# Delta stage: the sum of k's squares from two dense-format products, one state step later

## The chip, the cores and the metric

The kernel runs on one core of a Trainium2 chip. The metric is the device time of one execution in microseconds (us). A program of this size was executed three times for the median, and once more under the hardware profiler.

## The reference, cut to what matters

Two blocks follow each other on 512 rows of 1024 features; only the first layer of the first block, a gated delta rule over 8 heads, is touched. For each head the reference takes q, k and v from a projection, a causal convolution of 4 taps and a silu, and then

```python
def _l2norm(t):
    return t * lax.rsqrt(jnp.sum(t * t, axis=-1, keepdims=True) + EPS)
...
k = _l2norm(qkv[..., A_QK_WIDTH:2 * A_QK_WIDTH].reshape(bsz, seq, A_HEADS, A_HEAD_K).astype(f32))
v = qkv[..., 2 * A_QK_WIDTH:].reshape(bsz, seq, A_HEADS, A_HEAD_V).astype(f32)
...
v_new = u_c - jnp.einsum("bhcd,bhdv->bhcv", w_c, state)
o_c = jnp.einsum("bhcd,bhdv->bhcv", qd, state) + jnp.einsum("bhcj,bhjv->bhcv", a_c, v_new)
state = state * dec[..., None, None] + jnp.einsum("bhcd,bhcv->bhdv", ke, v_new)
```

The sum of k's squares over the 128 features of a head is what the change computes in another way.

## The kernel before, in words

Features lie on the partitions and the 512 positions along the rows. Large products split weight and activation into a high part, rounded to the dense format `F32R`, and a low part (the rest), and add three products (high by high, high by low, low by high). A weight tile comes by DMA into `wraw`, ScalarE casts its high part (`cast`), VectorE subtracts to get the low part (`low`), and each tile is 24 matmuls of 128x512.

The delta stage has a prologue and then one turn of `delta(i)` for each of 8 heads: a hardware loop for heads 1 to 5, written out for 0, 6 (`last_qkv`) and 7 (`last`). Each engine has its own list of instructions, in an order written by hand, and works through it strictly in turn; semaphores tie the lists together. In turn i TensorE solves the triangular systems of head i (`levels`), then goes through four chunks of 128 positions (t = 0 to 3), each of which needs the state that the last one left. The gaps of both are filled with matmuls of projection tiles (`strips`, L613). The lists `BEFORE_STATE`, `AFTER_KS`, `AFTER_V` and `AFTER_S` say how many filler matmuls follow each step; whatever is left of the 48 is done after the state steps, so their number in a turn is fixed.

A state step t > 0 goes round four engines' lists like this:

- TensorE: k by state (L784) and state by q (L785), fillers, then `tt` by `rr` (L792); later `kend` by `vn` (L803) and `vn` by the decayed products (L804), fillers.
- VectorE: `rr` (L1976) after L784; the new `state` (L1987 for t = 0, L1990 after) after L803.
- ScalarE: `vn` (L1354) after L792, which releases L803.

Between these steps VectorE and ScalarE do the work for head i+1. ScalarE scales the newest tap of each convolution (`conv_newest`, L1254), applies silu, squares k into `sq[:, 1, :]` (`square_k`, L1268), casts a weight tile (L1170), switches its table (L1365), exponentiates the decay (L1308) and takes the inverse root of the sum for k (`k_norms`, L1302, L1304). VectorE adds the three older taps (`conv_older`, L1782) and prepares the decay exponents (`exponent`, L1859). The sum of k's squares itself is `sums_of_k` (L692 to L695): one float32 matmul of a matrix of ones (`ones`) by `sq[:, 1, :]` into `pa[:, 1, :]`, which the trace records as two passes of 128x512. It stands behind L792 in step t = 1, where `AFTER_V[1]` is 0:

```python
                    if t == 1 and not last:
                        sums_of_k(i + 1)
                    if not last:
                        fill(after_v[t])
```

For head 0 the same function is called alone, ahead of the first strips, and in VectorE's list the fitting place is between L1842 and `conv_older(-1, 3, 0)`:

```python
            sums_of_k(0)
            strips(s, 0, (0, 1), 0, 3 * KD)
```

Later in the prologue TensorE turns k (L700), forms the products of k and q (L712), turns v (L706), spreads the small systems (L718) and starts `levels(0)` with L733, which waits for VectorE's `tn`.

The names that matter below: `rqk` holds the inverse root, `kn` (L1849) the unit k, `state_ready`, `r_ready`, `vn_ready`, `v_done` the semaphores of the state steps.

Of the kernel before, what the change touches and what calls it, by code (L numbers as in the profile page):

```python
# [13 lines left out]
F32 = mybir.dt.float32  # L14
# [5 lines left out]
P = 128  # L20
# [104 lines left out]
def build(nc, xT, w8, w11, w_gates, consts, vecs, a_log, dt_bias, rel_flip, ln_gb, w_spat, b_spat, outT,  # L125
# [5 lines left out]
    with ctx:  # L131
# [31 lines left out]
        def ev(name):  # L163

            if name not in made:
                made[name] = ctx.enter_context(nc.semaphore(name))
            return made[name]
# [30 lines left out]
        o_hi = r.sb("o_hi", [P, HA, S], F32R)  # L198
        o_lo = r.sb("o_lo", [P, HA, S], F32R)
        ys = r.sb("ys", [P, 4, S])  # L200
        sq = r.sb("sq", [P, 2, S])
        rqk = r.sb("rqk", [P, S])
        own = Region(r.at)
        r.at += 3 * P * 4
# [17 lines left out]
        tt = r.sb("tt", [P, NC, P])  # L222
        xm = r.sb("xm", [P, NC, P])
        xm32 = r.sb("xm32", [P, NC, 32])
        kend = r.sb("kend", [P, NC, P])
        bv = r.sb("bv", [P, NC, P])
        rr = r.sb("rr", [P, NC, P])
# [348 lines left out]
        def _(pe):  # L576
# [114 lines left out]

            def sums_of_k(i):  # L692

                pe.wait_ge(ev("k_squared"), i + 1)
                mm(pa[:, 1, :], ones, sq[:, 1, :], start=True, stop=True).then_inc(ev("k_sums"), 1)  # L695

            def turn_k(i):
                pe.wait_ge(ev("kn_ready"), i + 1)
# [63 lines left out]
            def delta(i, last, last_qkv=False):  # L762
# [17 lines left out]
                for t in range(NC):  # L780
                    q = slice(t * P, t * P + P)
                    if t > 0:
                        pe.wait_ge(ev("state_ready"), i * (NC - 1) + t)
                        mm(pb[:, q], kn[:, q], state[:], start=True, stop=True).then_inc(ev("ks_done"), 1)  # L784
                        mm(acc[:, 2, q], state[:], qe[:, q], start=True, stop=False)  # L785
                        if t == 3 and last:
                            pe.wait_ge(ev("q_squared"), i + 1)
                            mm(pd[:], ones, sq[:, 0, :], start=True, stop=False)
                        if not last:
                            fill(after_ks[t])  # L790
                        pe.wait_ge(ev("r_ready"), i * (NC - 1) + t)
                        mm(pc[:, q], tt[:, t, :], rr[:, t, :], start=True, stop=True).then_inc(ev("v_done"), 1)  # L792
                    else:
                        mm(pc[:, q], tt[:, t, :], bv[:, t, :], start=True, stop=True).then_inc(ev("v_done"), 1)
                    if t == 1 and not last:
                        sums_of_k(i + 1)
                    if not last:
                        fill(after_v[t])
                    elif t in (1, 2, 3):
                        fill(1)  # L800
                    pe.wait_ge(ev("vn_ready"), i * NC + (t + 1))
                    if t < NC - 1:
                        mm(pd[:, q], kend[:, t, :], vn[:, t, :], start=True, stop=True).then_inc(ev("s_done"), 1)  # L803
                    m = mm(acc[:, 2, q], vn[:, t, :], gd[:, t, 1, :], start=(t == 0), stop=True)  # L804
                    if t == NC - 1:
                        m.then_inc(ev("o_done"), 1)
                    if not last:
                        fill(after_s[t])
# [354 lines left out]
        def _(act):  # L1163
# [102 lines left out]
            def square_k(i):  # L1266
                act.wait_ge(ev("qkv_silu"), i * 3 + 5)
                A(sq[:, 1, :], ys[:, 1, :], ACT.Square).then_inc(ev("k_squared"), 1)  # L1268

            def square_q(i):  # L1270
                act.wait_ge(ev("qkv_silu"), i * 3 + 1)
# [5 lines left out]
            gates = pb[:, 0:64].rearrange("p (t c) -> p c t", c=16)  # L1277
            A(t0[:], gates[:, 0:8, :], ACT.Exp, scale=-1.0).then_inc(ev("gate_act"), 1)
            act.wait_ge(ev("consts_landed"), 32)
            conv_newest(1, 0, -1)  # L1280
            act.wait_ge(ev("gate_dve"), at(GATE_DVE, "gate_abs"))
            A(t1[:], t1[:], ACT.Exp, scale=-1.0).then_inc(ev("gate_act"), 1)
# [52 lines left out]
            def delta(i, last, last_qkv=False):  # L1335
# [19 lines left out]

                vn_of(0)
                if not last:
                    square_k(i)
                    conv_newest(3, i + 1, i)
                    act.wait_ge(acc_done, s.number(i, 3) + 1)  # L1360
                    cast(o, 0, 2) if last_qkv else cast(s, i + 1, 1)
                vn_of(1)
# [194 lines left out]
            def stick():  # L1557
# [12 lines left out]
                for step in range(blocks + 3):  # L1570
# [15 lines left out]
                    if step < blocks:  # L1586
                        k = 3 - v
                        g = slice(SEG[k], SEG[k] + (4 - k) * P)
                        act.wait_ge(ev("z_masked"), step + 1)
                        A(sw[:, :, g], zs[:, :, g], ACT.Abs).then_inc(ev("z_abs"), 1)  # L1590
                        act.wait_ge(ev("z_abs"), step + 1)
                        A(sw[:, :, g], sw[:, :, g], ACT.Exp, scale=-1.0).then_inc(ev("z_exp"), 1)
                        act.wait_ge(ev("z_exp"), step + 1)
                        A(sw[:, :, g], sw[:, :, g], ACT.Ln, bias=1.0).then_inc(ev("z_ln"), 1)
                    if 0 < i < SBP and v == 0:
                        turned_v(i)
                        cast_ahead(s, i, 2, i == SBP - 1)
# [106 lines left out]
        def _(dve):  # L1704
# [135 lines left out]
            dve.wait_ge(ev("solve_dve"), 7)  # L1840
            ts_(en[:], e8[:], -1.0, None, ALU.mult).then_inc(ev("solve_dve"), 1)
            nc.vector.memset(yx[:, :, 0:1], 1.0).then_inc(ev("solve_dve"), 1)  # L1842
            conv_older(-1, 3, 0)


            def unit_qk(i):

# [68 lines left out]
            def delta(i, last, last_qkv=False):  # L1916
# [55 lines left out]
                for t in range(NC):  # L1972
                    q = slice(t * P, t * P + P)
                    if t > 0:
                        dve.wait_ge(ev("ks_done"), i * (NC - 1) + t)
                        stt(rr[:, t, :], pb[:, q], nbe[:, i, t:t + 1], bv[:, t, :], ALU.mult, ALU.add  # L1976
                            ).then_inc(ev("r_ready"), 1)
                        if t == 1 and not last:
                            conv_older(i, 3, i + 1, (2, 3))
                        if t == 2 and last_qkv:  # L1980
                            low_after(o, 2, 1)
                        elif t == 2 and not last:
                            low(s, i + 1, 1)
                    if t < NC - 1:
                        dve.wait_ge(ev("s_done"), i * (NC - 1) + (t + 1))
                        if t == 0:
                            nc.vector.tensor_copy(state[:], pd[:, q]).then_inc(ev("state_ready"), 1)  # L1987
                        else:
                            dve.wait_ge(ev("state_ready"), i * (NC - 1) + t)
                            stt(state[:], state[:], ecl[:, i, t:t + 1], pd[:, q], ALU.mult, ALU.add  # L1990
                                ).then_inc(ev("state_ready"), 1)
                        if t == 0 and not last:
                            conv_older(i, 3, i + 1, (1,))
                        if t == 1 and not last:
                            exponent(i + 1)
# [230 lines left out]
            def stick():  # L2226
# [19 lines left out]
                for step in range(blocks + 3):  # L2246
# [7 lines left out]
                    if 1 <= step < blocks + 1:  # L2254
                        k = 3 - (step - 1) % NC
                        g = slice(SEG[k], SEG[k] + (4 - k) * P)
                        dve.wait_ge(ev("z_ln"), step)
                        x = stt(sp[:, :, g], zs[:, :, g], 0.0, sw[:, :, g], ALU.max, ALU.add)
                        if k < 3:
                            x.then_inc(ev("sp_whole"), 1)  # L2260
# [266 lines left out]
```

## Time and profile before

| what | us |
|---|---|
| median of 3 executions | 1793.81 |
| lowest, highest | 1793.61, 1793.97 |
| the profiled execution's own time | 1793.58 |
| its span, first to last instruction | 1791.9 |
| TensorE busy | 1761.8 (98%) |
| VectorE busy | 1153.6 (64%) |
| ScalarE busy | 845.8 (47%) |
| mean granted clock of TensorE | 0.998 |

A busy TensorE is the union of its records, whose ends are modelled; a matmul record is longer than its share of the engine, since neighbours overlap. What a matmul costs is read from the distance between starts, or from the chain of waits, which counts each moment once. The profile names TensorE's array PE, its weight loads PEld, VectorE DVE, ScalarE ACT and GpSimd POOL. "idle before <- X" is the time in which the engine stood before that instruction, and X is what ended it.

The eight heads span roughly 56 to 360 us of the 1791.9; the rest of the program is not touched except for three semaphores of the second block's attention that become one (`z_steps`), with the same waits.

### The profile page before, as it was taken

The page shows a single profiled execution, that of the slowest core. Times are in us where ns is not written, and L with a number is a line of the kernel's source. Part 1 is how long each engine was busy: PE and PEld are TensorE (multiplying, and loading weights), DVE is VectorE, ACT ScalarE, POOL GpSimd, SP SyncE. Part 2 cuts the span into 40 slices and gives each one's busy share as a digit, 9 for nine tenths or more (in the row PEclk, how much of TensorE's full clock was granted, in tenths as well). Part 3 has the DMA queues.
Part 4 walks back from the last instruction along what each step waited for, and adds up shares of the span by engine and source line. Part 5 has one row for each costly group of instructions (what it writes and reads, how often), then busy time and mean ns, then how long its engine had stood idle before and what let it go on. Part 6 is the DMA issues. An engine that isn't in the chain of part 4 may idle for free.

```text
span 1791.9 us, 23591 instructions
## 1 busy us (share of the span) xinstructions
PE 1761.8 (98%) x8174; PEld 1388.8 (78%) x8174; DVE 1153.6 (64%) x1826; ACT 845.8 (47%) x1311; POOL 34.4 (2%) x61
## 2 busy tenths in 40 slices
PE   9999999899999999999999999999999999999998
PEld 6787777678888888888887788888887765677886
DVE  7888888567777743377777677776433556665444
ACT  6555555444444432267777444444322465643222
POOL 1000000000000000000000000000000000100000
PEclk9999999999999999999999999999999999999999
DMA  5522122022222142143331222222321312223221
GB/s 198 167 70 70 59 70 59 36 96 95 93 94 93 59 155 88 62 132 106 103 114 65 94 94 94 94 94 84 124 97 52 106 36 71 92 78 99 100 93 60
DMA packets 45816, 163.26 MB, mean 91 GB/s; under 512 B 5841, under 2 KB 8164, under 8 KB 45760
## 3 DMA queue, kind: packets, MB, share of 16 engines
q1 hardware_dynamic: 40864, 148.00, 24.7%
q0 software_dynamic: 4464, 14.47, 2.9%
q8 instruction: 32, 0.52, 0.1%
q14 instruction: 24, 0.20, 0.0%
q10 hardware_dynamic: 432, 0.07, 0.0%
HBM read 155.89 MB, written 6.63 MB: 91 GB/s over the span
## 4 chain that ended last, share of the span: by engine, by line
PE 91%; DVE 4%; ACT 3%; issue 1%; DMA 0%; SPq 0%; DVEq 0%; ACTq 0%
PE acc L587 23%; PE acc L588 23%; PE acc L589 23%; PE acc L613 8%; ACT wsplit L1170 1%; PE pbc L750 1%; PE pbc L954 1%; PE pbc L733 1%; PE pa L587 1%; PE pa L588 1%; PE pa L589 1%; DVE wsplit L1712 1%; PE pbc L1029 1%; PE pa L712 1%; PE pd L967 1%
## 5 line engine op out<-in xcount | busy, mean ns | idle before, releaser
L587 PE MATMUL acc<-xhi,wsplit 128*128 128x512 f32 x1200 | 487.5, 406 | 1.4 <-DVE at_vs L2155 1.3
L1170 ACT ACTIVATE wsplit<-wraw 128x1024 fp32r<-128x1024 f32 (+1 forms) x252 | 276.3, 1097 | 442.6 <-PE acc L589 408.6
L589 PE MATMUL acc<-xhi,wsplit 128*128 128x512 f32 x1200 | 475.5, 396 | 0.0
L588 PE MATMUL acc<-xlo,wsplit 128*128 128x512 f32 x1200 | 475.5, 396 | 0.0
L1712 DVE TENSOR_TENSOR wsplit<-wraw,wsplit 128x1024 fp32r<-128x1024 f32 (+1 forms) x249 | 317.0, 1274 | 158.9 <-ACT wsplit L1170 158.0
L587 PEld LDWEIGHTS acc<-xhi,wsplit 128*128 128x128 f32 x1200 | 225.9, 188 | 68.7 <-issue 14.0
L589 PEld LDWEIGHTS acc<-xhi,wsplit 128*128 128x128 f32 x1200 | 225.9, 188 | 54.7
L588 PEld LDWEIGHTS acc<-xlo,wsplit 128*128 128x128 f32 x1200 | 226.4, 189 | 51.4 <-issue 1.4
L613 PE MATMUL acc<-xhi,wsplit 128*128 128x512 f32 x464 | 157.8, 412 | 0.0
L588 PE MATMUL acc<-hid_lo,wsplit 128*128 128x512 f32 x352 | 139.6, 396 | 0.0
L589 PE MATMUL acc<-hid_hi,wsplit 128*128 128x512 f32 x352 | 139.6, 396 | 0.0
L587 PE MATMUL acc<-hid_hi,wsplit 128*128 128x512 f32 x352 | 139.5, 396 | 0.0
L2114 DVE TENSOR_TENSOR tmp<-acc,rstd 128x512 f32<-128x512 f32 x88 | 60.5, 688 | 65.7 <-PE acc L589 57.8
L613 PE MATMUL acc<-xlo,wsplit 128*128 128x512 f32 x232 | 98.8, 426 | 0.0
L613 PEld LDWEIGHTS acc<-xhi,wsplit 128*128 128x128 f32 x464 | 84.0, 189 | 15.9 <-issue 1.9
L2077 DVE TENSOR_TENSOR h<-h,acc 128x512 f32<-128x512 f32 (+2 forms) x38 | 25.8, 680 | 107.2 <-PE acc L589 107.2
L1469 ACT ACTIVATE hid_hi<-fy 128x512 f32 (+1 forms) x44 | 27.8, 633 | 110.0 <-DVE fy L2125 110.0
L1462 ACT ACTIVATE fy<-tmp,vec 128x512 f32<-128x512 f32 x88 | 71.1, 808 | 17.0 <-DVE tmp L2114 17.0
L587 PEld LDWEIGHTS acc<-hid_hi,wsplit 128*128 128x128 f32 x352 | 66.3, 188 | 16.2
L589 PEld LDWEIGHTS acc<-hid_hi,wsplit 128*128 128x128 f32 x352 | 66.3, 188 | 16.2
L588 PEld LDWEIGHTS acc<-hid_lo,wsplit 128*128 128x128 f32 x352 | 66.3, 188 | 16.2
L2120 DVE SCALAR_TENSOR_TENSOR fy<-tmp,vec,fy 128x510 f32<-128x510 f32 x88 | 66.0, 750 | 12.0 <-DVE fy L2117 3.1
(390 smaller groups left out, 2542.2 us busy)
## 6 DMA issues: line engine op xcount, KB each, us to landing
wraw<-w SPq DMA_DIRECT2D x220, 512.0 KB, 3.3
wraw<-w SPq DMA_DIRECT2D x32, 704.0 KB, 4.1
bias_dram<-ext_dram POOLq DMA_DIRECT2D x1, 4096.0 KB, 20.8
bias<-bias_dram POOLq DMA_DIRECT2D x16, 256.0 KB, 3.0
at_ks<-at_ks SPq DMA_DIRECT2D x16, 256.0 KB, 2.9
crow<-row_dram POOLq DMA_DIRECT2D x8, 256.0 KB, 3.8
brow<-row_dram POOLq DMA_DIRECT2D x8, 256.0 KB, 4.3
h<-xT SPq DMA_DIRECT2D x3, 512.0 KB, 8.2
```

What stands on the lines that cost most here:

```text
L587: mm(out, whi[:, k, :], a[:, x_at + k, :], start=(k == first), stop=False)
L588: mm(out, whi[:, k, :], b[:, x_at + k, :], start=False, stop=False)
L589: m = mm(out, wlo[:, k, :], a[:, x_at + k, :], start=False, stop=(k == last))
L613: d = mm(bank(s, i, j), w[:, k, :], x[:, k, :], start=(m == 0), stop=(m == 3 * KD - 1))
L712: m = mm(pa[:, t // 2, (t % 2) * 2 * P:(t % 2 + 1) * 2 * P], kn[:, t * P:t * P + P], kq[:, t, :, :].rearrange("p a q -> p (a q)"), start=T ...
L1170: A(split(s, i, j, 0), raw(s, j), ACT.Copy).then_inc(w_hi_ready, 1)
L1462: A(fy[:, j, :], tmp[:, j % 2, :], ACT.Identity, scale=w[:, g, f, 2:3], bias=wb[:, g, f, :]).then_inc(ev("ffn_newest"), 1)
L1469: A(hid_hi[:, f, :], fy[:, j, :], ACT.Copy).then_inc(ev("hid_hi_ready"), 1)
L1712: tt_(split(s, i, j, 1), raw(s, j), split(s, i, j, 0).bitcast(F32), ALU.subtract).then_inc(w_lo_ready, 1)
L2077: tt_(h[:, i * per + m, cols], h[:, i * per + m, cols], out, ALU.add).then_inc(acc_free, 1 if s.kc == KD else 2)
L2114: tt_(tmp[:, j % 2, :], acc[:, j % 2, :], rstd[:], ALU.mult).then_inc(acc_free, 1)
L2120: stt(fy[:, j, 2:S], tmp[:, j % 2, 0:S - 2], w[:, g, f, 0:1], fy[:, j, 2:S], ALU.mult, ALU.add).then_inc(ev("ffn_conv"), 1)
```

## The change

`sums_of_k` becomes two `F32R` matmuls, of a dense matrix of ones by a high part `k_hi` and a low part `k_lo` of the squares. `k_hi` is a second `Square` on ScalarE, written in the dense format over the place of `rqk`; `k_lo` is a subtraction on VectorE, written in place over `sq[:, 1, :]`. In TensorE's list the sum moves from step t = 1 (behind L792) to step t = 2 (behind L784 and L785, ahead of the fillers `after_ks[2]`). In VectorE's list the subtraction comes behind `rr` of step t = 1, ahead of v's taps 2 and 3 and of the new state. In ScalarE's list `conv_newest(3, ...)` now precedes the two squares. A copy makes the dense ones in the prologue, where the subtraction for head 0 stands behind L1842.

```diff
--- before.py
+++ after.py
@@ -198,7 +198,9 @@
         o_hi = r.sb("o_hi", [P, HA, S], F32R)
         o_lo = r.sb("o_lo", [P, HA, S], F32R)
         ys = r.sb("ys", [P, 4, S])
+        k_lo = sb("k_lo", [P, S], F32R, at=r.at + S * 4)
         sq = r.sb("sq", [P, 2, S])
+        k_hi = sb("k_hi", [P, S], F32R, at=r.at)
         rqk = r.sb("rqk", [P, S])
         own = Region(r.at)
         r.at += 3 * P * 4
@@ -222,6 +224,7 @@
         tt = r.sb("tt", [P, NC, P])
         xm = r.sb("xm", [P, NC, P])
         xm32 = r.sb("xm32", [P, NC, 32])
+        ones_r = r.sb("ones_r", [P, P], F32R)
         kend = r.sb("kend", [P, NC, P])
         bv = r.sb("bv", [P, NC, P])
         rr = r.sb("rr", [P, NC, P])
@@ -691,8 +694,9 @@
 
             def sums_of_k(i):
 
-                pe.wait_ge(ev("k_squared"), i + 1)
-                mm(pa[:, 1, :], ones, sq[:, 1, :], start=True, stop=True).then_inc(ev("k_sums"), 1)
+                pe.wait_ge(ev("k_low_ready"), i + 1)
+                mm(pa[:, 1, :], ones_r[:], k_hi[:], start=True, stop=False)
+                mm(pa[:, 1, :], ones_r[:], k_lo[:], start=False, stop=True).then_inc(ev("k_sums"), 1)
 
             def turn_k(i):
                 pe.wait_ge(ev("kn_ready"), i + 1)
@@ -786,14 +790,14 @@
                         if t == 3 and last:
                             pe.wait_ge(ev("q_squared"), i + 1)
                             mm(pd[:], ones, sq[:, 0, :], start=True, stop=False)
+                        if t == 2 and not last:
+                            sums_of_k(i + 1)
                         if not last:
                             fill(after_ks[t])
                         pe.wait_ge(ev("r_ready"), i * (NC - 1) + t)
                         mm(pc[:, q], tt[:, t, :], rr[:, t, :], start=True, stop=True).then_inc(ev("v_done"), 1)
                     else:
                         mm(pc[:, q], tt[:, t, :], bv[:, t, :], start=True, stop=True).then_inc(ev("v_done"), 1)
-                    if t == 1 and not last:
-                        sums_of_k(i + 1)
                     if not last:
                         fill(after_v[t])
                     elif t in (1, 2, 3):
@@ -1266,6 +1270,7 @@
             def square_k(i):
                 act.wait_ge(ev("qkv_silu"), i * 3 + 5)
                 A(sq[:, 1, :], ys[:, 1, :], ACT.Square).then_inc(ev("k_squared"), 1)
+                A(k_hi[:], ys[:, 1, :], ACT.Square).then_inc(ev("k_squared"), 1)
 
             def square_q(i):
                 act.wait_ge(ev("qkv_silu"), i * 3 + 1)
@@ -1277,6 +1282,7 @@
             gates = pb[:, 0:64].rearrange("p (t c) -> p c t", c=16)
             A(t0[:], gates[:, 0:8, :], ACT.Exp, scale=-1.0).then_inc(ev("gate_act"), 1)
             act.wait_ge(ev("consts_landed"), 32)
+            A(ones_r[:], ones, ACT.Copy)
             conv_newest(1, 0, -1)
             act.wait_ge(ev("gate_dve"), at(GATE_DVE, "gate_abs"))
             A(t1[:], t1[:], ACT.Exp, scale=-1.0).then_inc(ev("gate_act"), 1)
@@ -1355,8 +1361,8 @@
 
                 vn_of(0)
                 if not last:
+                    conv_newest(3, i + 1, i)
                     square_k(i)
-                    conv_newest(3, i + 1, i)
                     act.wait_ge(acc_done, s.number(i, 3) + 1)
                     cast(o, 0, 2) if last_qkv else cast(s, i + 1, 1)
                 vn_of(1)
@@ -1587,11 +1593,11 @@
                         k = 3 - v
                         g = slice(SEG[k], SEG[k] + (4 - k) * P)
                         act.wait_ge(ev("z_masked"), step + 1)
-                        A(sw[:, :, g], zs[:, :, g], ACT.Abs).then_inc(ev("z_abs"), 1)
-                        act.wait_ge(ev("z_abs"), step + 1)
-                        A(sw[:, :, g], sw[:, :, g], ACT.Exp, scale=-1.0).then_inc(ev("z_exp"), 1)
-                        act.wait_ge(ev("z_exp"), step + 1)
-                        A(sw[:, :, g], sw[:, :, g], ACT.Ln, bias=1.0).then_inc(ev("z_ln"), 1)
+                        A(sw[:, :, g], zs[:, :, g], ACT.Abs).then_inc(ev("z_steps"), 1)
+                        act.wait_ge(ev("z_steps"), 3 * step + 1)
+                        A(sw[:, :, g], sw[:, :, g], ACT.Exp, scale=-1.0).then_inc(ev("z_steps"), 1)
+                        act.wait_ge(ev("z_steps"), 3 * step + 2)
+                        A(sw[:, :, g], sw[:, :, g], ACT.Ln, bias=1.0).then_inc(ev("z_steps"), 1)
                     if 0 < i < SBP and v == 0:
                         turned_v(i)
                         cast_ahead(s, i, 2, i == SBP - 1)
@@ -1840,8 +1846,14 @@
             dve.wait_ge(ev("solve_dve"), 7)
             ts_(en[:], e8[:], -1.0, None, ALU.mult).then_inc(ev("solve_dve"), 1)
             nc.vector.memset(yx[:, :, 0:1], 1.0).then_inc(ev("solve_dve"), 1)
+            dve.wait_ge(ev("k_squared"), 2)
+            tt_(k_lo[:], sq[:, 1, :], k_hi[:].bitcast(F32), ALU.subtract).then_inc(ev("k_low_ready"), 1)
             conv_older(-1, 3, 0)
 
+            def low_of_k(i):
+
+                dve.wait_ge(ev("k_squared"), 2 * i + 2)
+                tt_(k_lo[:], sq[:, 1, :], k_hi[:].bitcast(F32), ALU.subtract).then_inc(ev("k_low_ready"), 1)
 
             def unit_qk(i):
 
@@ -1976,6 +1988,7 @@
                         stt(rr[:, t, :], pb[:, q], nbe[:, i, t:t + 1], bv[:, t, :], ALU.mult, ALU.add
                             ).then_inc(ev("r_ready"), 1)
                         if t == 1 and not last:
+                            low_of_k(i + 1)
                             conv_older(i, 3, i + 1, (2, 3))
                         if t == 2 and last_qkv:
                             low_after(o, 2, 1)
@@ -2254,7 +2267,7 @@
                     if 1 <= step < blocks + 1:
                         k = 3 - (step - 1) % NC
                         g = slice(SEG[k], SEG[k] + (4 - k) * P)
-                        dve.wait_ge(ev("z_ln"), step)
+                        dve.wait_ge(ev("z_steps"), 3 * step)
                         x = stt(sp[:, :, g], zs[:, :, g], 0.0, sw[:, :, g], ALU.max, ALU.add)
                         if k < 3:
                             x.then_inc(ev("sp_whole"), 1)
```

## Rows read from the trace of the kernel before

**Rows 1.** One turn: us; PE, PEld, DVE, ACT, POOL busy (x); PEclk, DMA, GB/s.

```profile
89.70:128.36 38.66, 38.50 (x218) 30.68 (x217) 33.83 (x63) 20.59 (x38) 1.07 (x2) 1.00 0.22 68
```

**Rows 2.** Chain that ended last, in order of time: start us, us, what.

```profile
90.29 4.67 PE acc L613 x20
...
114.25 0.86 PE pa L695 x2
```

**Rows 3.** Timeline of ScalarE: start us, us, engine, line, operation, tiles [idle before].

```profile
111.31 0.62 ACT L1268 ACTIVATE sq<-ys 128x512 f32<-128x512 f32 x1
...
111.83 0.71 ACT L1254 ACTIVATE ys<-tmp,vec 128x512 f32<-128x512 f32 x1
...
112.45 1.05 ACT L1170 ACTIVATE wsplit<-wraw 128x1024 fp32r<-128x1024 f32 x1
...
114.28 0.28 ACT L1354 ACTIVATE vn<-pbc 128x128 f32<-128x128 f32 x1 [0.79 <-PE pbc L792]
...
115.29 0.63 ACT L1263 ACTIVATE ys<-ys 128x512 f32<-128x512 f32 x1 [0.73 <-DVE ys L1782]
...
117.77 0.26 ACT L1354 ACTIVATE vn<-pbc 128x128 f32<-128x128 f32 x1
```

**Rows 4.** Timeline of VectorE in the same state steps.

```profile
112.00 0.29 DVE L1987 COPY state<-pd 128x128 f32<-128x128 f32 x1 [0.81 <-PE pd L803]
...
112.69 0.75 DVE L1782 SCALAR_TENSOR_TENSOR ys<-tmp,vec,ys 128x511 f32<-128x511 f32 x1 [0.40 <-ACT ys L1254]
...
113.36 0.34 DVE L1976 SCALAR_TENSOR_TENSOR rr<-pbc,nbe,bv 128x128 f32<-128x128 f32 x1
...
113.62 1.63 DVE L1782 SCALAR_TENSOR_TENSOR ys<-tmp,vec,ys 128x510 f32<-128x510 f32 x2
...
115.46 0.35 DVE L1990 SCALAR_TENSOR_TENSOR state<-state,ecl,pd 128x128 f32<-128x128 f32 x1 [0.20 <-PE pd L803]
...
115.72 1.13 DVE L1859 SCALAR_TENSOR_TENSOR dec<-crow,cc,cst 128x128 f32<-128x128 f32 x4
...
116.77 0.34 DVE L1976 SCALAR_TENSOR_TENSOR rr<-pbc,nbe,bv 128x128 f32<-128x128 f32 x1
```

**Rows 5.** Timeline of TensorE (PE) and its weight loads (PEld), with what followed.

```profile
112.71 0.38 PE L784 MATMUL pbc<-state,kn 128*128 128x128 f32 x2
...
113.76 0.30 PEld L792 LDWEIGHTS pbc<-rr,tt 128*128 128x128 f32 x2 [0.41 <-DVE rr L1976]
...
114.61 0.52 PEld L803 LDWEIGHTS pd<-vn,kend 128*128 128x128 f32 x2 [0.33 <-ACT vn L1354]
...
116.09 0.38 PE L784 MATMUL pbc<-state,kn 128*128 128x128 f32 x2
...
117.23 0.43 PE L792 MATMUL pbc<-rr,tt 128*128 128x128 f32 x2
...
119.34 0.38 PE L784 MATMUL pbc<-state,kn 128*128 128x128 f32 x2
...
119.87 0.35 DVE L1976 SCALAR_TENSOR_TENSOR rr<-pbc,nbe,bv 128x128 f32<-128x128 f32 x1 [0.81 <-PE pbc L784]
```

**Rows 6.** Groups by line, the first 300 us: busy us, mean ns, idle before.

```profile
L2039 DVE TENSOR_TENSOR o_lo<-oy,o_hi 128x512 f32 x5 | 3.4, 685 | 0.0
```

**Rows 7.** Timeline of the prologue, ahead of the first head.

```profile
36.42 1.12 PE L695 MATMUL pa<-sq,cst 128*128 128x512 f32 x2 [0.28 <-ACT sq L1268]
...
38.99 0.74 DVE L1782 SCALAR_TENSOR_TENSOR ys<-tmp,vec,ys 128x511 f32<-128x511 f32 x1
...
47.11 0.66 PE L706 MATMUL pbc<-cst,ys 128*128 128x128 f32 x4 [0.32 <-ACT ys L1263]
...
56.65 1.16 PE L733 MATMUL pbc<-tn,gd 128*128 128x128 f32 x8 [0.97 <-DVE tn L1902]
```

**Rows 8.** Groups by line: the matmuls that open the program.

```profile
L638 PE MATMUL pd<-rr 128*128 128x512 f32 x14 | 9.2, 828 | 1.5 <-POOL rr L505 1.5
```

**Rows 9.** Waits of TensorE in the whole span: us in total, times, longest us.

```profile
PE pbc L1029 <- DVE sp L2263: 4.5, 4, 1.8
```

## Prediction

> **What bounds the kernel now.** I read the engine totals first, then the windows by turn of the head loop, the chain of waits, and the timeline of one turn. A turn takes 38.66 us, of which TensorE is busy 38.50, VectorE 33.83 and ScalarE 20.59, at a granted clock of 1.00 [rows 1]. TensorE is the bound, but as a list worked through in order: what lengthens a turn is either a matmul more or a wait that no filler covers. The chain of waits is nearly all TensorE and gives the two prices that matter: 20 dense fillers take 4.67 us, 0.234 each, and the present sum of k's squares takes 0.86 for its two passes [rows 2]. The timeline of a state step then shows who comes last. The reader is to see there that in step t = 1 three lists run almost level: VectorE waits only 0.20 before the new state [rows 4], TensorE waits 0.33 for `vn` in its weight loads and nothing in its matmuls, because the sum covers it [rows 5], and ScalarE is free 0.79 before `vn` [rows 3]. The other turns of the loop repeat this to 0.02 us; I take one and multiply.
>
> **TensorE's own work.** The sum goes from 0.86 to 2 x 0.234 = 0.47: 0.39 saved a head. But the old sum stood where TensorE would otherwise wait for `vn`, so the time saved there is only worth what the new order makes of it. I follow it step by step, with the present times in brackets.
>
> **ScalarE in a turn.** `conv_newest` takes the square's place and starts at 111.31 (111.83), so it ends at about 112.03. Each square then costs 0.52 of the list (111.83 - 111.31) [rows 3]: one square more. The cast starts at 111.31 + 0.62 + 0.52 + 0.52 = 112.97 (112.45) and ends at 114.02. `vn` starts at 114.16 at the earliest (below), so this is covered, by 0.14 only.
>
> **VectorE in a turn.** The first tap can now follow the state copy at once, at about 112.25 (112.69, with 0.40 of waiting) [rows 4]. `rr` is then no longer held by the tap but by L784: from 119.34 to 119.87, where VectorE stood idle, it is 0.53, hence 112.71 + 0.53 = 113.24 (113.36) [rows 4, 5]. So the earlier tap gains 0.12, not 0.40. Behind `rr` comes the new subtraction, an operation like L2039, 0.685 long [rows 6]; neighbours in this list start about 0.08 before the end of the one before (the tap is 0.75 long and `rr` starts 0.67 after it [rows 4]), which leaves 0.61. It pushes taps 2 and 3, and with them the new state. Today the list is free for the state at about 115.17, some 0.08 before the taps end at 113.62 + 1.63 = 115.25, and the state starts at 115.46. Now it is 115.17 - 0.12 + 0.61 = 115.66: of the 0.49 of delay the slack before the state takes 0.29, and it starts 0.20 later than today.
>
> **TensorE in a turn.** L792 follows `rr` by 0.40: 113.64 (113.76) [rows 5]. `vn` follows by 0.52, 114.16 (114.28), and L803 by 0.33 more, 114.49. With L803, L804 and three fillers (1.14, as from 116.09 to 117.23) TensorE would be ready for L784 at 115.63, but the state comes later: 115.66 + 0.40 = 116.06 (116.09). So the 0.86 taken out of the place behind L792 turns into waiting: about 0.5 before L803 and 0.4 before L784. Behind L784 and L785 come the two new matmuls in front of the three fillers: 116.06 + 0.10 (a weight load that is not ahead of its matmul) + 0.44 + 0.47 + 0.70 = 117.77 for L792. Today's is 117.28 (the row's 117.23 with a record 0.05 longer than usual) [rows 5]. That is **0.5 late**. `rr` of this step is not the bound: the exponents follow the state, 115.66 + (116.77 - 115.46) = 116.97, plus 0.40 = 117.37.
>
> ScalarE says the same by another way. Its silu of v follows the taps at 115.29, and silu, table switch and decay reach `vn` at 117.77, 2.48 later, without a pause [rows 3]. Taps 0.49 late make that 118.26, again **0.5 late**. Two chains that agree are why I hold this term firmly. From there to the end of the turn TensorE, VectorE and ScalarE all start from this point, fillers and solve are as before, and the inverse root for k, though its sum now comes a step later, starts behind `vn` of t = 2 as today. No slack takes the half microsecond back. Bounds for a turn: 0.29 (only what is left of the subtraction after the 0.12 and the 0.20 of waiting) and 0.65 (if the squares and cast overrun `vn` as well). Loop turns and head 0: 6 x 0.50 = 3.0. In the seventh the filler lists are shorter and the two matmuls fall into a wait, while ScalarE's chain stays: 0.4. The last has no next k.
>
> **The prologue.** `sums_of_k(0)` stands in front of the strips, so TensorE does nothing until the low part exists. The last product is through at 36.14 and the sum starts at 36.42 today, the strips at 36.42 + 0.10 + 0.86 = 37.38 [rows 7]. The subtraction takes the place of the tap at 38.99: 38.99 + 0.69 + 0.06 + 0.10 + 0.47 = 40.31 for the first strip, **2.9 late**. The root, the unit k and its product with beta (four operations of about 0.7, until 43.2) hide behind the 24 strips (5.6, until 45.9). The wait of 0.32 for silu of v before L706 disappears, with its exposed load about 0.45: 2.5 late. The 0.97 before L733 does not help, since `tn` comes from a solve that starts from TensorE's own L718. The copy that makes the dense ones stands before a `conv_newest` on which the gates' path hangs; it costs between 0 and 0.28 (a 128x128 operation, `vn` [rows 3]), I take 0.15. Together **2.6**, bounds 2.2 and 3.4.
>
> `z_steps` counts the same waits on one semaphore: nothing moves, 0. No DMA and no step of SP or POOL is moved; their waits hang on steps that shift with the rest.
>
> **The sum.** 3.0 + 0.4 + 2.6 = 6.0 us. The profiled execution took 1793.58, its span 1791.9, so the span becomes 1797.9 and the execution 1799.6; the median of the three is 0.23 above the profiled one, so 1799.8.
>
> **Rival 1, not slower: TensorE's list decides.** If the state of step t = 1 were not held by VectorE, L792 of t = 2 would come no later than today and the turn would save the 0.39 of the sum and the 0.12 of the earlier `rr`: 7 x 0.51 = 3.6 less, with the prologue's 2.6 a net 1.0 less, 1792.8. Its place is the new state behind the taps; it decides if that starts by 115.23 (115.63 - 0.40) rather than at 115.66, which takes a subtraction of under 0.2 instead of 0.61. For it: VectorE has 0.40 and 0.20 of waiting here. Against it: both were spent above, and ScalarE's chain would have to give way too. 0.07.
>
> **Rival 2: the turns come out even.** The delays and savings cancel and only the prologue's stall is paid: 1796.4. It needs slack between t = 2 and the next solve, where the rows show almost none. 0.12.
>
> **Rival 3: the clock.** The new stall in the prologue, from 36.14 to about 39.9, is 3.8 long; the longest wait of TensorE today is 1.8, at a mean granted clock of 0.998 [rows 9]. The program opens with 14 passes that take 9.2, 828 ns each, behind an idle engine [rows 8]; at the 0.43 apart of the sum's passes they would take 6.0. If the stall brings such a stretch back, it costs about 3.1 more: 1802.9. The row of the opening is no proof, as the profile prints no lower clock there. The Trainium skill, "TensorE: Matmul & The Clock Gate", section "HAM oscillation — how this bites in real kernels", warns that a long enough idle gap between bursts puts the engine back to half its clock; by that rule this rival would come true. No trace here has such a gap inside the work. 0.11.
>
> **Rival 4: the change does not do what it says.** If the dense products with ones and squares ran like the float32 passes, 0.43 each, the sum would cost 0.86 as before, now behind L784: 7 x 0.39 more, 1802.5. Every dense row has 0.234, so 0.03.
>
> **The numbers.** The forecast has 0.67. About 0.2% (3.6 us) is what a measurement of this kernel can tell from no change. Slower by more: forecast, rivals 3 and 4, less a little for a prologue and turns both at their lower bounds: 0.78. Within: rivals 1 and 2 and that rest, 0.19. Faster by more: 0.03. The forecast's own bounds are 2.2 + 7 x 0.29 = 4.2 and 3.4 + 7 x 0.65 = 8.0. The range goes from rival 2 to rival 3.
>
> **What would show it.** In the profile after: TensorE idle for some 3.5 us before the sum at about 40, waiting for VectorE; turns of 39.2 us instead of 38.66, with TensorE waiting for `vn` before L803 and for the state before L784 in t = 1, and the state's wait of 0.20 for L803 gone. Turns of 38.2 would mean rival 1, of 38.66 rival 2; fillers 0.43 apart behind the stall rival 3. I am wrong in the mechanism if VectorE still waits for L803 in step t = 1, or if the solve starts no later in the turn than today.

## Result and the profile after

The changed kernel takes 1800.68 us (median of 6 runs, 1800.53 to 1801.92), the kernel before 1793.71 (6 runs, 1793.61 to 1793.97). The ratio is 1.0039, 95% interval 1.0028 to 1.005: 7.0 us slower. The profiled execution took 1800.6, its span is 1798.9 (before 1791.9).

The page's totals of the changed kernel, span and busy time by engine:

```profile
span 1798.9 us, 23612 instructions
...
PE 1762.5 (98%) x8174; PEld 1390.4 (77%) x8174; DVE 1158.4 (64%) x1834; ACT 852.2 (47%) x1320; POOL 34.5 (2%) x61
```

TensorE is busy 0.7 us more although it has 8 x 0.39 less to do; a stretch at half clock, below, is in that number. The rest of the 7.0 us is waiting. The waits of TensorE (us in total, times, longest us) name it, beside [rows 9]:

```profile
PE pbc L1033 <- DVE sp L2276: 4.5, 4, 1.8
PE pa L698 <- DVE k_lo L1850: 3.5, 1, 3.5
PE pd L807 <- ACT vn L1360: 3.2, 9, 0.4
...
PE pbc L788 <- DVE state L2003: 1.3, 7, 0.2
```

One wait of 3.5 for head 0's low part (L698 is the first dense product of the sum, L1850 the subtraction) is new, and the waits for `vn` in front of L807 (L803 before) have grown from 0.4 to 3.2 in all.

**The prologue.** Timeline of the changed kernel, answering to [rows 7]:

```profile
39.07 0.68 DVE L1850 TENSOR_TENSOR k_lo<-sq,k_hi 128x512 fp32r<-128x512 f32 x1
...
39.81 0.50 PE L698 MATMUL pa<-k_hi,ones_r 128*128 128x512 f32 x1 [3.54 <-DVE k_lo L1850]
...
40.38 0.39 PE L616 MATMUL acc<-xhi,wsplit 128*128 128x512 f32 x1
...
42.17 1.05 PE L616 MATMUL acc<-xhi,wsplit 128*128 128x512 f32 x2
...
47.53 0.60 PE L704 MATMUL pbc<-cst,kn 128*128 128x128 f32 x4
...
60.58 1.16 PE L737 MATMUL pbc<-tn,gd 128*128 128x128 f32 x8 [0.97 <-DVE tn L1914]
```

The strips start at 40.38 instead of 37.38. Between 40.9 and 44.2 neighbours among them are 0.43 apart, behind it 0.234 again. The windows of the changed kernel (stretch, length, then busy and count of PE, PEld, DVE, ACT, POOL, the granted clock, DMA share, GB/s) say why:

```profile
38.00:39.80 1.80, 0.00 (x0) 0.00 (x0) 1.73 (x8) 1.04 (x2) 0.00 (x0) 1.00 0.85 320
39.80:40.60 0.80, 0.79 (x3) 0.67 (x4) 0.77 (x2) 0.00 (x0) 0.00 (x0) 1.00 0.17 63
...
41.50:42.50 1.00, 1.00 (x4) 0.81 (x3) 0.84 (x2) 1.00 (x2) 0.65 (x1) 0.50 0.00 0
...
44.30:46.00 1.70, 1.70 (x9) 1.38 (x8) 1.68 (x4) 1.12 (x2) 0.00 (x0) 1.00 1.01 342
```

The granted clock is 1.00 when TensorE resumes, then 0.50, the lower of its two levels (1.2 of 2.4 GHz), from 40.8 to 44.2, and 1.00 from there on. The engine had done nothing from 36.3 to 39.8 and was busy all through the slow stretch. L704 (L700 before) starts at 47.53, 4.54 late against 42.99 in the trace of before: 3.0 from the late start, 1.5 from the clock. Of this 0.6 is taken back at the wait for silu of v, which is gone, and L737 (L733) is 3.93 late, with its wait of 0.97 unchanged.

**The turns.** The matmul that spreads the small systems comes once a turn, at the same point of TensorE's list; in the changed kernel:

```profile
94.09 0.59 PE L722 MATMUL pa<-xm,cst 128*128 128x256 f32 x2
...
133.25 0.59 PE L722 MATMUL pa<-xm,cst 128*128 128x256 f32 x2
```

39.16 apart, against 38.66 [rows 1]. Head 0's turn adds 0.46, each of the five of the loop 0.50, the seventh 0.27. With the prologue that is 3.93 + 0.46 + 2.5 + 0.27 = 7.2; 0.2 of it is taken back in later stages. The step where it happens, timeline of the changed kernel, against [rows 3 to 5] (all 4.38 later to begin with: L788, the old L784, starts at 117.09 instead of 112.71):

```profile
117.61 0.35 DVE L1988 SCALAR_TENSOR_TENSOR rr<-pbc,nbe,bv 128x128 f32<-128x128 f32 x1 [0.29 <-PE pbc L788]
117.88 0.68 DVE L1856 TENSOR_TENSOR k_lo<-sq,k_hi 128x512 fp32r<-128x512 f32 x1
...
118.02 0.49 PE L798 MATMUL pbc<-rr,tt 128*128 128x128 f32 x2
...
118.88 0.49 PE L807 MATMUL pd<-vn,kend 128*128 128x128 f32 x2 [0.37 <-ACT vn L1360]
...
120.04 0.34 DVE L2003 SCALAR_TENSOR_TENSOR state<-state,ecl,pd 128x128 f32<-128x128 f32 x1
120.16 0.63 ACT L1267 ACTIVATE ys<-ys 128x512 f32<-128x512 f32 x1 [1.33 <-DVE ys L1788]
...
120.44 0.49 PE L788 MATMUL pbc<-state,kn 128*128 128x128 f32 x2 [0.16 <-DVE state L2003]
...
120.91 0.47 PE L698 MATMUL pa<-k_hi,ones_r 128*128 128x512 f32 x1
...
122.16 0.38 PE L798 MATMUL pbc<-rr,tt 128*128 128x128 f32 x2
...
122.64 0.26 ACT L1360 ACTIVATE vn<-pbc 128x128 f32<-128x128 f32 x1
```

With 4.38 taken off, and the forecast in brackets: `rr` at 113.23 (113.24), L798 at 113.64 (113.64), L807 at 114.50 (114.49), silu at 115.78 (115.78), the state at 115.66 (115.66), L788 at 116.06 (116.06), L798 of t = 2 at 117.78 (117.77), `vn` at 118.26 (118.26). L807 waits 0.37 and L788 another 0.16 in the matmuls, and the sum sits in front of the fillers.

### The profile page after: what moved, and what is told of

The parts are those of the page before. It is cut to its first block, busy times and chain, and to the rows that moved or that the text cites. A ratio compares the mean times of both kernels' runs of the same rounds, so it can differ in the third digit from the quotient of the medians.

```text
span 1798.9 us, 23612 instructions
## 1 busy us (share of the span) xinstructions
PE 1762.5 (98%) x8174; PEld 1390.4 (77%) x8174; DVE 1158.4 (64%) x1834; ACT 852.2 (47%) x1320; POOL 34.5 (2%) x61
## 4 chain that ended last, share of the span: by engine, by line
PE 91%; DVE 4%; ACT 3%; issue 1%; DMA 0%; DVEq 0%; SPq 0%; ACTq 0%
PE acc L590 23%; PE acc L591 23%; PE acc L592 23%; PE acc L616 9%; ACT wsplit L1174 1%; PE pbc L754 1%; PE pbc L958 1%; PE pbc L737 1%; PE pa L592 1%; PE pa L591 1%; PE pa L590 1%; PE pa L716 1%; PE pd L971 1%; DVE wsplit L1718 1%; PE pbc L1033 1%
```

## Experiments

Ten kernels were run. Two theories stood against each other at first: **A**, that the prologue costs 3.9 (late low part 2.4, clock 1.5) and the turns 0.5 each, and **B**, that the prologue's stall is mostly absorbed and the turns cost about 1.0 each.

### Head 0's sum as before

`first_sum_of_k` is the float32 matmul of before; it waits for the first square only.

```diff
-            sums_of_k(0)
+            first_sum_of_k()
...
-            dve.wait_ge(ev("k_squared"), 2)
-            tt_(k_lo[:], sq[:, 1, :], k_hi[:].bitcast(F32), ALU.subtract).then_inc(ev("k_low_ready"), 1)
             conv_older(-1, 3, 0)
```

> The changed kernel with only head 0's sum of k's squares taken back to the float32 product, as soon as the first square is there; turns as changed. Theory A (the prologue's wait of 3.5 us for the subtraction, and the stretch at half the granted clock behind it, cost 3.9 of the 7.0; the turns 0.5 each): the wait goes, the clock stays at 1.00, the opening copy of the ones (about 0.15) stays, so about 1797.0 and no run a microsecond above the others. Theory B (the prologue costs little that is not absorbed, the turns cost 1.0 each): 1800 or more.

Measured: 1796.92 median of 11 runs (ratio to before 1.0019, interval 1.0009 to 1.0028), granted clock 1.00 throughout the prologue of its trace. 3.8 less than the change: the prologue's share is 3.8 of the 7.0, theory B is out. The runs spread from 1796.1 to 1798.2, but so did those of the kernel before in that session (1793.3 to 1795.4), so the spread tells nothing.

### The stall filled with spare matmuls

```diff
+            for n in range(13):
+                mm(pd[:], xhi[:, 0, 0:P], xhi[:, n % KD, :], start=True, stop=True)
             sums_of_k(0)
```

> The changed kernel with 13 spare dense matmuls (results unused, 3.0 us) in TensorE's list in front of the first sum, where it waits. Theory A (it is the idleness of TensorE that lowers its clock afterwards): the sum still starts at about 39.8 us, but the granted clock stays at 1.00 and the strips behind are 0.234 apart, so 1.3 us less than the changed kernel, about 1799.3, and the runs lie closer together than the 1800.5 to 1801.9 of the change. Theory B (the slow stretch comes from other engines or transfers at that time): fillers 0.43 apart as before, 1800.6.

Measured: 1799.6 median of 6 (1.0032, 1.002 to 1.0044). TensorE's timeline in it:

```profile
39.66 0.50 PE L698 MATMUL pa<-k_hi,ones_r 128*128 128x512 f32 x1 [0.58 <-DVE k_lo L1852]
...
45.85 0.60 PE L704 MATMUL pbc<-cst,kn 128*128 128x128 f32 x4
```

and the window behind the sum:

```profile
42.00:43.00 1.00, 1.00 (x6) 0.82 (x5) 0.97 (x2) 0.82 (x1) 0.11 (x1) 1.00 0.18 25
```

The sum waits for the same subtraction and starts within 0.15 of the same time, but from it to L704 are 6.19 us instead of 7.72 (39.81 to 47.53), and the clock is 1.00. The lists of the other engines are unchanged. The gain of 1.1 in the median is near the 1.3 forecast for the clock; that the runs would lie closer together was not seen. One trace at full clock is little by itself (the last section has one that keeps it after the long wait too), but over all traces the count at this place is clear: with the wait of 3.5 in front of the sum four of five show a stretch at 0.50 around it, without it none of seven.

Elsewhere the clock falls in this trace all the same, in a matmul of the second block's attention:

```profile
1518.73 3.48 PE L1035 MATMUL pbc<-sp,order 128*128 128x512 f32 x4 [1.78 <-DVE sp L2278]
...
1520.00:1521.00 1.00, 1.00 (x2) 0.34 (x1) 0.00 (x0) 0.97 (x4) 0.00 (x0) 0.50 0.00 0
```

It is 0.50 from 1519.1 to 1522.5, and the four passes take 3.48, in the changed kernel (L1033) 1.98. So the 1.5 won in the prologue was lost again in this one execution (1799.95 against the 1800.6 of the changed kernel's), and the times show the gain only over several executions: the lowest of the six is 1798.91, the lowest of the change 1800.53.

### The first subtraction moved up

```diff
             take(-1, 3)
+            dve.wait_ge(ev("k_squared"), 2)
+            tt_(k_lo[:], sq[:, 1, :], k_hi[:].bitcast(F32), ALU.subtract).then_inc(ev("k_low_ready"), 1)
...
-            dve.wait_ge(ev("k_squared"), 2)
-            tt_(k_lo[:], sq[:, 1, :], k_hi[:].bitcast(F32), ALU.subtract).then_inc(ev("k_low_ready"), 1)
             conv_older(-1, 3, 0)
```

> The changed kernel with head 0's subtraction moved up in VectorE's list, right behind the taking of v's tile. Theory A: it runs at about 37.05, the sum starts near 37.8, a wait of about 1.5 instead of 3.5; the clock does not fall; 2.0 less for the start and 1.3 less for the clock: about 1797.4. Theory B (any wait of a microsecond or more there lowers the clock): 1798.7.

Measured: 1797.36 median of 11 (1.002, 1.0011 to 1.0029). The wait in front of the sum:

```profile
PE pa L698 <- DVE k_lo L1835: 1.5, 1, 1.5
```

1.5, with the granted clock at 1.00 behind it: 3.3 less than the change. One line, moved in VectorE's list, gives back nearly all that the prologue cost.

### v's newest tap first, alone

```diff
-                    square_k(i)
                     conv_newest(3, i + 1, i)
+                    square_k(i)
```

on the kernel before.

> The kernel before with one edit: v's newest tap in front of the square of k on ScalarE. By the step of the prediction, rr of step t = 1 comes 0.12 us earlier (bound by L784 instead of the tap) and the taps too, so 7 x 0.12 = 0.8 less than before: about 1792.9, turns of 38.54. The rival is that another wait of the turn takes it back: 1793.7.

Measured: turns of 38.565 (for instance 129.97 to 168.53), 0.10 shorter than before; 1793.02 median of 11, ratio 0.9998, interval 0.9989 to 1.0007. The turn shows the gain, the time alone does not. One reason stands in its trace, which took 1794.35, and has to do with none of its edits; in the opening:

```profile
13.43 0.50 PE L645 MATMUL acc<-xhi,wg_hi 128*128 128x512 f32 x1 [1.84 <-DVE xlo L1736]
...
16.00:17.00 1.00, 1.00 (x4) 0.81 (x3) 1.00 (x2) 1.00 (x2) 0.00 (x0) 0.50 1.03 406
```

From 14.9 to 18.3 the clock is 0.50, which costs about 1.5 (nine matmuls take 3.64 from start to start, in the trace of before about 2.08). The eleven runs fall into two groups, six at 1791.8 to 1793.0 and five at 1794.2 to 1794.6, of which the traced one is one; that the other four have such a stretch too is not shown.

### Which chain makes the turns long: three kernels

First the dense sum back in step t = 1 (in the changed kernel `sums_of_k(i + 1)` under `if t == 1 and not last` behind L798, as before), then the decay behind the root, then both.

```diff
-                if not last:
-                    decay(i + 1)
                 vn_of(2)
                 if not last:
                     k_norms(i + 1)
+                    decay(i + 1)
```

> The changed kernel with the two dense products back in step t = 1, where the float32 one stood, so that the wait for vn is partly covered again; subtraction, squares and copy as changed. Measured by the length of a turn (38.66 before, 39.16 changed). If TensorE's chain alone made the half microsecond (new state late, two matmuls behind it), L792's successor in t = 2 comes back to about where it was and the turn to 38.7. If the second chain is as long (subtraction, taps, silu, table switch, decay, vn of t = 2 on ScalarE), the turn stays at 39.15.

> The changed kernel with ScalarE's decay exponential moved from in front of vn of t = 2 to behind the inverse root for k: 0.54 us less ahead of that vn, nothing else. If ScalarE's chain alone made the half microsecond, the turn goes from 39.16 to about 38.66. If TensorE's is as long, it stays at 39.15.

> Both edits of the two runs beside it. If the two chains are equal and independent, each edit alone does nothing and both together bring the turn back to about 38.68. If the subtraction on VectorE is a third bound by itself, it stays near 39.1.

Measured, each in one profiled execution, the same matmul as above in two neighbouring turns; the sum back in t = 1:

```profile
94.17 0.59 PE L722 MATMUL pa<-xm,cst 128*128 128x256 f32 x2
...
133.32 0.59 PE L722 MATMUL pa<-xm,cst 128*128 128x256 f32 x2
```

the decay moved:

```profile
94.87 0.59 PE L722 MATMUL pa<-xm,cst 128*128 128x256 f32 x2
...
134.06 0.59 PE L722 MATMUL pa<-xm,cst 128*128 128x256 f32 x2
```

both:

```profile
94.90 0.59 PE L722 MATMUL pa<-xm,cst 128*128 128x256 f32 x2
...
133.77 0.59 PE L722 MATMUL pa<-xm,cst 128*128 128x256 f32 x2
```

Turns of 39.15, 39.19 and 38.87 (the single executions took 1800.4, 1800.87 and 1799.4, with stretches at half clock of different length in the prologue, see the last section). Each edit alone does nothing, both together give 0.3: the two chains are independent and equally long, as the prediction has it. The 38.68 expected of both is not reached; 0.2 are left. What holds L796 there is read from the timeline, and no kernel takes it away by itself: a third, shorter bound, VectorE's own list.

```profile
120.88 0.34 DVE L2002 SCALAR_TENSOR_TENSOR state<-state,ecl,pd 128x128 f32<-128x128 f32 x1
...
121.14 1.13 DVE L1870 SCALAR_TENSOR_TENSOR dec<-crow,cc,cst 128x128 f32<-128x128 f32 x4
...
122.19 0.35 DVE L1987 SCALAR_TENSOR_TENSOR rr<-pbc,nbe,bv 128x128 f32<-128x128 f32 x1
...
122.58 0.30 PEld L796 LDWEIGHTS pbc<-rr,tt 128*128 128x128 f32 x2 [0.34 <-DVE rr L1987]
```

`L788` starts at 117.92 there, 5.21 later than in [rows 5]; without those, the state is at 115.67, `rr` of t = 2 at 116.98 (116.77 before) and L796 (L792 before) at 117.37, where 117.28 was the time before, with its weight load exposed: the pair takes 0.49 instead of 0.38. The 0.09 and the 0.11 are the 0.2.

### The subtraction behind the state, and the move alone

```diff
                         if t == 1 and not last:
-                            low_of_k(i + 1)
                             conv_older(i, 3, i + 1, (2, 3))
...
                         if t == 1 and not last:
+                            low_of_k(i + 1)
                             exponent(i + 1)
```

> The changed kernel with one edit in the turns: VectorE's subtraction stands behind the new state of step t = 1 instead of in front of taps 2 and 3. If its place in VectorE's list is what makes the turns long, the taps and the state come 0.6 earlier, and what is left is the exponents 0.6 later, so that rr of t = 2 holds L792 by about 0.1: turns of 38.75 instead of 39.16. If the second square on ScalarE or the two matmuls in front of the fillers make them long, 39.1.

Measured: turns of 38.93 (92.45 to 131.37, then 170.31); its one execution took 1797.34, the kernel before beside it 1793.21. Half of the half microsecond comes back, not four fifths. Timeline:

```profile
117.86 0.35 DVE L2002 SCALAR_TENSOR_TENSOR state<-state,ecl,pd 128x128 f32<-128x128 f32 x1
...
119.78 0.35 DVE L1988 SCALAR_TENSOR_TENSOR rr<-pbc,nbe,bv 128x128 f32<-128x128 f32 x1
...
120.18 0.49 PE L798 MATMUL pbc<-rr,tt 128*128 128x128 f32 x2
...
121.21 0.38 PE L807 MATMUL pd<-vn,kend 128*128 128x128 f32 x2
```

With the offset of 2.75 off (L788 at 115.46), L798 starts at 117.43 and L807 of t = 2 at 118.46, 0.26 late against 118.20 before. The expectation had left out that TensorE loads weights in the open, about 0.1 (a pair of 0.49 instead of 0.38), after the waits that it really runs into here.

The move alone, with the float32 sum and none of the new operations, on the kernel with v's tap first:

```diff
+                        if t == 2 and not last:
+                            sums_of_k(i + 1)
...
-                    if t == 1 and not last:
-                        sums_of_k(i + 1)
```

> The kernel before with v's newest tap first and its float32 sum moved behind L784 and L785 of step t = 2; no second square, no subtraction, no dense products. It prices the move alone, against turns of 38.565 with the tap alone. The 0.86 of the sum no longer covers the wait for vn in t = 1 and stands in front of the fillers in t = 2: by the prediction's arithmetic L784 at 115.63, L792 at 115.63 + 0.44 + 0.86 + 0.70 = 117.63 instead of 117.28, turns of 39.0. If the cover was worth nothing, 38.6.

Measured: turns of 39.13 (90.10 to 129.22, then 168.36), against 38.565 with the sum in its old place: 0.57 for the move alone, 0.13 more than the 0.44 computed; its one execution took 1795.98 against 1793.21. Its wait for `vn`, in the same trace:

```profile
114.88 0.49 PE L803 MATMUL pd<-vn,kend 128*128 128x128 f32 x2 [0.37 <-ACT vn L1354]
...
116.57 1.02 PE L695 MATMUL pa<-sq,cst 128*128 128x512 f32 x2
...
118.12 0.38 PE L794 MATMUL pbc<-rr,tt 128*128 128x128 f32 x2
```

These prices do not add up to the change, since the chains run side by side. Where the subtraction stands behind the state, the dense sum makes the moved turn 0.20 shorter (38.93 against 39.13), not 0.39. With the subtraction in front of the taps the turn is 39.16 whether the sum is moved or not (39.15 above), so in the change itself the move alone decides nothing. The sum back in t = 1 together with the subtraction behind the state was not run by itself.

### A version that uses the dense sum

```diff
-            BEFORE_STATE, AFTER_KS, AFTER_V, AFTER_S = 2, [0, 2, 3, 3], [3, 0, 3, 3], [3, 3, 3, 0]
-            LAST_BEFORE_STATE, LAST_AFTER_KS, LAST_AFTER_V, LAST_AFTER_S = 3, [0, 1, 1, 1], [2, 0, 2, 1], [2, 2, 1, 0]
+            BEFORE_STATE, AFTER_KS, AFTER_V, AFTER_S = 2, [0, 2, 1, 3], [3, 2, 3, 3], [3, 3, 3, 0]
+            LAST_BEFORE_STATE, LAST_AFTER_KS, LAST_AFTER_V, LAST_AFTER_S = 3, [0, 1, 0, 1], [2, 1, 2, 1], [2, 2, 1, 0]
...
+            strips(s, 0, (0, 1), 0, 8)
             sums_of_k(0)
-            strips(s, 0, (0, 1), 0, 3 * KD)
+            strips(s, 0, (0, 1), 8, 3 * KD)
...
                         if t == 1 and not last:
-                            exponent(i + 1)
+                            low_of_k(i + 1)
+                        if t == 2 and not last:
+                            exponent(i + 1)
...
                         if t == 1 and not last:
-                            low_of_k(i + 1)
                             conv_older(i, 3, i + 1, (2, 3))
```

with the first subtraction moved up and the decay behind the root as above.

> A version meant to use the dense sum: head 0's subtraction early and its sum behind 8 strips; subtraction behind the new state instead of in front of it; exponents and decay a step later; two fillers moved behind L792's place in step t = 1, ahead of the wait for vn, and two fewer behind the sum in t = 2. By the same arithmetic vn of t = 2 is needed at 117.26 instead of 117.77 and L792 of t = 3 starts at 119.98 instead of 120.49: turns of about 38.15, 7 x 0.5 less than before, prologue level or 0.4 better. About 1790.2. If a list I have not followed (the third state waiting for the cast weight's low part, the root's) holds it, 1793 to 1794.

Measured: 1791.86 median of 11, the kernel before 1793.78 (15 runs); ratio 0.9989, interval 0.998 to 0.9998. It is 1.9 us below the kernel before, with an interval that ends at 0.9998, just below 1, and 8.8 below the change's median, which is of another series. In its trace:

```profile
128.42 0.59 PE L722 MATMUL pa<-xm,cst 128*128 128x256 f32 x2
...
166.78 0.59 PE L722 MATMUL pa<-xm,cst 128*128 128x256 f32 x2
```

Turns of 38.36, 0.30 shorter than before, of the 0.5 hoped for, and 2.2 less over the eight heads (from the spreading matmul of head 0 to that of head 7, 266.38 us against 268.57). The prologue is not level as hoped: L737 starts at 57.32, 0.67 later than before (56.65), since TensorE waits 0.57 for the unit k in front of L704 and 0.33 for silu of v in front of L710. Two steps are later than computed: `rr` of t = 3 waits behind the exponents (120.03 for an L788 at 119.34), and the fillers stand behind waits with open weight loads. Which of its edits brings how much was not separated.

## Why the prediction was right

The forecast was slower, 1799.8, range 1796.0 to 1803.2; measured 1800.68. By its steps:

- **ScalarE, VectorE, TensorE in a turn**: from `rr` to `vn` of t = 2 every start came within 0.02 of its forecast (the first tap at 112.20 for "about 112.25"), and the turn is 0.50 longer. The claim that two chains carry it is shown by the three kernels of one and both edits. The third bound, VectorE alone, the text had only as a start that is "0.20 later than today"; with the other two removed it still costs 0.2 a turn.
- **Head 0 and the seventh turn**: 0.46 and 0.27 for 0.50 and 0.4. Turns together 3.2 for 3.4.
- **The prologue's stall**: the strips are 3.0 late for 2.9, and 3.93 - 1.5 = 2.4 remain for 2.6. The opening copy cannot be told apart: 0.13 in this pair of traces for the 0.15, but traces that share the change's opening differ by 0.3 among themselves (the sum starts at 39.78 to 40.09). At silu of v 0.61 came back, not 0.45.
- **The clock** is the step that failed: the forecast left it at 1.00 and held rival 3 at 0.11. It fell, and cost 1.5 us, not 3.1. So the sum, 6.0, was 1.0 short of 7.0, all of it and a little more the clock. The rival named the place and the cause rightly; its chance was too small for a gap twice the longest that the trace of before had, and its size, taken from the program's opening, was twice what came here (1.3 to 2.6 in the four traces that slowed). How near the number came is in part luck of the execution: had the clock held, as in one trace of five, the same kernel would have taken about 1799.2 (1800.68 - 1.5, an estimate), and in two of the five it lost about one more.
- The Trainium skill, "TensorE: Matmul & The Clock Gate", section "HAM oscillation — how this bites in real kernels", says that a long idle gap between bursts halves the clock afterwards. The traces agree in the main: 0.50 around the end of an idle gap of 3.5 us in four of the five that have it. They also show it behind waits of only 1.8 us, in two places.
- **Rivals 1, 2 and 4** did not come: turns of 39.16, not 38.2 or 38.66, and the two dense products 0.31 and 0.23 apart from their neighbours, not 0.43.

## What to carry to other kernels

A matmul that is cheaper is worth something only where nothing waits: before moving or shrinking it, look at which wait it covers. In a hand-ordered kernel put a new helper operation behind whatever releases the bounding engine, not at the first moment its inputs are ready, and check the peeled first turn by itself, since an operation that has a place in the loop may have none there. If an edit alone changes nothing, try it with the edit for the next chain of equal length.

## What the hardware did that was not expected

The same wait of 3.54 us at the same point is followed by quite different stretches at half clock. Five kernels share that prologue; from the start of the sum to L704, 6.19 us at full clock:

| kernel | sum to L704, us | more than 6.19 |
|---|---|---|
| subtraction behind the state | 6.19 | 0.0 |
| dense sum in t = 1 | 7.54 | 1.35 |
| the change | 7.72 | 1.53 |
| decay behind the root | 8.53 | 2.34 |
| both edits | 8.75 | 2.56 |

The windows (columns as above) of the kernel with the subtraction behind the state, which did not slow down, and of the one with both edits, which was slow from 38.75, before TensorE resumed at 39.9, until 45.6:

```profile
42.00:43.00 1.00, 1.00 (x6) 0.81 (x5) 0.81 (x3) 1.00 (x2) 0.24 (x1) 1.00 0.07 16
```

```profile
39.00:40.00 1.00, 0.10 (x1) 0.10 (x1) 0.97 (x5) 0.13 (x1) 0.00 (x0) 0.50 0.90 366
...
42.00:43.00 1.00, 1.00 (x3) 0.77 (x3) 0.36 (x2) 1.00 (x2) 0.28 (x1) 0.50 0.05 8
...
46.00:47.00 1.00, 1.00 (x6) 0.79 (x5) 0.56 (x1) 0.98 (x3) 0.00 (x0) 1.00 1.04 340
```

None of their edits touches the prologue, so this is a matter of the single execution. The stretches at 0.50 come in two lengths: 3.4 us (the change, dense sum in t = 1) and 6.8 us (decay behind the root, both edits). The fall does not wait for work: in three of the four it comes while TensorE is still idle, 0.4 to 1.6 before the sum, and in the change 1.0 after the sum has started.

Nor does it need a wait of 3.5. The stretches of the filled stall (1519.1 to 1522.5) and of v's tap alone (14.9 to 18.3), shown above, are 3.4 long too and follow waits of 1.78 and 1.84. The first of these waits stands in all twelve traces, at the same place, and in one alone the clock falls behind it. With a wait of 1.5 in front of the sum (one trace), or of 0.6 (one trace), the clock stayed at 1.00 there. So in these traces it is a matter of chance, high behind 3.5 us of idleness (four of five) and low behind 1.8 (one of twelve at that place).

Two of the change's six runs are more than 0.8 us above the others (1801.63 and 1801.92, mean granted clock 0.997 and 0.996, against 1800.53 to 1800.77). They left no trace, and a longer stretch in the prologue is only one reading: of 28 runs of the kernel before, which has no such wait, six lie 0.7 to 1.6 above the median of 1793.76.
